# Dealing the taps of a depthwise convolution differently between a projection's products, with state stores issued later and filler products of other widths

## The chip, the cores and the metric

The kernel runs on one core of a Trainium2 chip. The metric is the device time of one execution in microseconds (us); lower is better. The kernel before takes 1147.51 us (median of 3 runs, 1146.17 to 1147.53).

## What is computed

One layer of a decoder trunk, for a prompt of 1024 tokens and 8 sample tokens, so N = 1032 columns of D = 1024 channels:

```
h = rmsnorm(x, norm1_g) * (1 + sc1) + sh1          # sc, sh, g come from silu(c) @ w_ada + b_ada
z = h @ w_in;  u, gb, gc, v, ga, gg = split(z)     # widths 256, 384, 384, 384, 384, 384
ya = pool_mix(u)                                   # causal means over 2, 4, 8, 16 rows, small product
yb = gb * causal_dwconv(gc * v, width 3)
yc = silu(layernorm(causal_dwconv(ga * sigmoid(gg), width 31) + conf_b))
x = x + g1 * (concat(ya, yb, yc) @ w_out)
h = rmsnorm(x, norm2_g) * (1 + sc2) + sh2
x = x + g2 * (square(relu(h @ w_ff1)) @ w_ff2)
y = rmsnorm(x, final_g)
```

The last rows of u, of gc * v and of ga * sigmoid(gg) are stored as new states.

## The kernel before, in words

Activations lie transposed in SBUF: channels on the 128 partitions, 1032 tokens on the free axis, in three column tiles of 344 (`TW`). A matrix product is made in float32r with both operands split in a high and a low part: for each block of 128 input channels three products (high by high, high by low, low by high), each over 3 tiles, so 9 matmuls of 128x344 per block. `product` (L1224 to L1235) does this; the two PSUM halves of `acc` (three banks each) take the chunks in turn, so a product may start when the chunk two before it was read.

`plan()` fixes the order of the units (one unit is one load of 128 weight columns). First gg and ga for c = 0, 1, 2; then u for c = 0, 1; then v, gc, gb for c = 0, 1, 2; then the output projection in two parts: `p1` (8 units of 5 blocks, over ya and yb) and `p2` (4 units of 3 blocks by two, over yc). Behind that come the second norm and the feed-forward part. The weights of a unit go from DMA to `wraw`, from there by ACT to `whi` (`high`, L531) and by POOL to `wlo` (`low`, L456): one ACT and one POOL instruction for each unit. ACT may do that for unit u + 2 when the product of unit u has ended.

Between the products of one round of ga there are also the products that make the modulation (`modulate`, L1367, from `ada` and `cT` into `modps`). DVE copies `modps` away (`mod_to_rows`, L791); the first `modulate` of the next round waits for that copy. PE then transposes it (L1377) and DVE adds the bias (`mod_finish`, L800).

What DVE does for each unit is written out by hand in the loop from L974 on:
- ga: glu = product times sigmoid (L981, L984), which also frees the chunk.
- u: `pooled` (L911 to L929), `ya_low` (L939).
- gc: product times v, and the convolution of width 3 (L1011 to L1022) into `wk[2]`.
- gb: yb = product times `wk[2]` (L1026). ACT rounds it to `yab_hi` (L633), DVE subtracts to get `yab_lo` (L1029).

The convolution of width 31 is the filling between these. It has 96 steps, in `steps`: for each of 3 channel blocks one start with bias (L886), 30 taps of one multiply-add over some 1000 columns (L892), and one addition for the samples (L896). `convolve(n)` does the next n steps, in order, from where it stands. Its calls give the dealing: 14, 14, 7 behind ga; 4, 4 behind u; 7 behind each v; 5 behind each gc; 6, 6 and all the rest behind gb. After the last, DVE adds the three blocks up (L1034, L1035) for the mean of the layernorm.

The first `p1` product reads the five blocks of ya and yb in order; its block 4 is yb of c = 2, and before it PE waits for the `yab_lo` of that block:

```
if kind == "p1":
    if c == 0:
        ready = lambda k: pe.wait_ge(ylo_ready, k + 1)
```

On ACT, in the turn of `p1` with c = 5, stand 16 DMAs that store the new states (L638 to L648), ahead of the three copies that make `yc_hi` (L653). DVE makes `yc_lo` from it (L1064), for `p2`.

At the second norm PE has little to do: it sums squares over the partitions with matmuls of one column (`token_sums`, L1265), spreads the reciprocal roots over the partitions (`spread`, L1294), and waits. Between these stand filler products whose result is never read (`keep_clock`, L1275): `WARM = (7, 12, 23)` of them, each 128x344, all into the bank `modps`, in the three places given by

```
norm_sums(3, WARM[0])
keep_clock(WARM[1])
spread(3, CHUNK_AT["norm2"])
keep_clock(WARM[2])
```

`WARM[0]` lies between the two halves of the token sums, `WARM[1]` ahead of the spread, `WARM[2]` behind it.

Of the kernel before, what the change touches and what calls it, by code (L numbers as in the profile page):

```python
# [8 lines left out]
ACT = mybir.ActivationFunctionType  # L9
AX_X = mybir.AxisListType.X  # L10

P = 128
# [5 lines left out]
TW = N // NT  # L18
# [3 lines left out]
POOL_C, CONV_C = 2, 3  # L22
# [79 lines left out]
COLS_AHEAD = 3  # L102


WARM = (7, 12, 23)
LAG = 2
SQ = {2: 0, 3: CONV_C, 4: CONV_C + KD}
ADDED = {2: 0, 3: 1, 4: KD - 1}
# [2 lines left out]
def decoder_trunk(nc, x_prompt, x_sample, c_prompt, c_sample, state_pool, state_sconv, state_conf,  # L111
# [11 lines left out]
    with ctx:  # L123
# [145 lines left out]
        def tiled(ap):  # L269
            return ap.rearrange("p (t w) -> p t w", t=NT)  # L270
# [231 lines left out]
        def _(act):  # L502
# [84 lines left out]
            for u in range(U_FF):  # L587
                (kind, c), n = UNITS[u]
                ps = flat(chunk_of(n))
                if kind == "p2":  # L590
                    squares(3, 2 * c, FREED_V[CHUNK_AT[("p2", 2 * c)]])
                if kind == "p1" and c == 2:
                    for j in range(CONV_C):
                        act.wait_ge(centred, j + 1)
                        nc.scalar.activation(wk[j][:], dc[:, j, :], ACT.Square).then_inc(sq_ready, 1)
                if kind == "p1" and c == LN_ROOT:
                    root(2)
                if kind == "p1" and c == 5:
                    for j in range(CONV_C):
                        act.wait_ge(ln_scaled, j + 1)  # L600
                        if j == 2:
                            act.wait_ge(silu_ready, 1)
                        nc.scalar.activation(wk[1 + j % 2][:], dc[:, j, :], ACT.Sigmoid,
                                             bias=lbT[:, j:j + 1]).then_inc(lsig_ready, 1)
                high_of(u + 2)
                if kind == "gg":
                    if c:
                        act.wait_ge(glu_ready, c)
                    nc.scalar.activation(tiled(wk[2]), ps, ACT.Sigmoid).then_inc(sig_ready, 1)
                if kind == "gg" and c == 2:  # L610

                    act.dma_start(ns_pool[0, :, 0:PBUF - 1, :], state_pool[0, :, 1:PBUF, :]).then_inc(old_stored, 16)
                    act.dma_start(ns_sconv[0, :, 0:SK - 2, :], state_sconv[0, :, 1:SK - 1, :]).then_inc(old_stored, 16)
                    act.dma_start(ns_conf[0, :, 0:CK - 2, :], state_conf[0, :, 1:CK - 1, :]).then_inc(old_stored, 16)
                if kind == "u":
                    nc.scalar.activation(last_cols[:, 0, 23 * c:23 * c + 23],
                                         chunk_of(n)[:, 2, TW - 23:TW], ACT.Copy).then_inc(last_u, 1)
                    if c == 1:
                        act.wait_ge(pool_ready, 1)
                    nc.scalar.activation(tiled(wk[c]), ps, ACT.Copy).then_inc(u_ready, 1)  # L620
                    if c == 1:
                        ya_high(0)
                if kind == "v":
                    if c == 0:
                        act.wait_ge(pool_ready, 2)
                    else:
                        act.wait_ge(ylo_ready, POOL_C + c)
                    nc.scalar.activation(tiled(wk[0]), ps, ACT.Copy).then_inc(v_ready, 1)
                    if c == 0:
                        ya_high(1)  # L630
                if kind == "gb":
                    act.wait_ge(yb_ready, c + 1)
                    nc.scalar.activation(yab_hi[:, POOL_C + c, :], wk[0][:], ACT.Copy).then_inc(yhi_ready, 1)  # L633
                if kind == "p1" and c == 5:
                    act.wait_ge(states_ready, 1)
                    for j in range(POOL_C):
                        r, cols = 23 * j, slice(j * P, (j + 1) * P)
                        act.dma_start(np_pool[0, 0, :, cols], states_out[r:r + PBUF, 0, :]).then_inc(new_stored, 16)  # L638
                        act.dma_start(ns_pool[0, :, PBUF - 1, cols], states_out[r + PBUF:r + 23, 0, :]
                                      ).then_inc(new_stored, 16)  # L640
                    for j in range(CONV_C):
                        r, cols = 46 + 10 * j, slice(j * P, (j + 1) * P)
                        act.dma_start(np_sconv[0, 0, :, cols], states_out[r:r + 2, 0, :]).then_inc(new_stored, 16)
                        act.dma_start(ns_sconv[0, :, SK - 2, cols], states_out[r + 2:r + 10, 0, :]
                                      ).then_inc(new_stored, 16)
                        r = LASTC * j
                        act.dma_start(np_conf[0, 0, :, cols], states_out[r:r + CK - 1, 1, :]).then_inc(new_stored, 16)
                        act.dma_start(ns_conf[0, :, CK - 2, cols], states_out[r + CK - 1:r + LASTC, 1, :]  # L648
                                      ).then_inc(new_stored, 16)
                if kind == "p1" and c == 5:  # L650
                    for j in range(CONV_C):
                        act.wait_ge(silu_ready, j + 1)
                        nc.scalar.activation(yc_hi[:, j, :], dc[:, j, :], ACT.Copy).then_inc(yhi_ready, 1)  # L653
                if kind == "p2":
                    squares(3, 2 * c + 1, FREED_V[CHUNK_AT[("p2", 2 * c + 1)]])

# [69 lines left out]
        def _(dve):  # L726
# [248 lines left out]
            for u in range(U_FF):  # L975
                (kind, c), n = UNITS[u]
                ps = flat(chunk_of(n))
                if kind == "ga":
# [5 lines left out]
                    nc.vector.tensor_tensor(tiled(glu[:, c, :]), ps, tiled(wk[2]), ALU.mult).then_inc(glu_ready, 1)  # L984
                    if c == 2:
                        mod_to_rows(2)
                    convolve(14 if c < 2 else 7)
                if kind == "gg" and c == 1:
                    mod_to_rows(1)
                if kind == "gg" and c == 2:  # L990
# [1 line left out]
                if kind == "u":  # L992
# [5 lines left out]
                    pooled(c)  # L998
                    if c == 1:
                        ya_low(0)  # L1000
                    convolve(4)
                if kind == "v":
                    if c == 0:
                        ya_low(1)
                    convolve(7)
                if kind == "gc":
                    dve.wait_ge(psum_full, n + 1)
                    dve.wait_ge(v_ready, c + 1)
# [11 lines left out]
                        link(nc.vector.scalar_tensor_tensor(out[:, s:T], cv[:, 0:T - s], tap[2 - s], out[:, s:T],  # L1020
                                                            ALU.mult, ALU.add))
                    link(nc.vector.tensor_tensor(out[:, T:N], out[:, T:N], past_sconv[:, c, :], ALU.add))  # L1022
                    convolve(5)
                if kind == "gb":
                    dve.wait_ge(psum_full, n + 1)
                    nc.vector.tensor_tensor(tiled(wk[0]), ps, tiled(wk[2]), ALU.mult).then_inc(yb_ready, 1)  # L1026
                    dve.wait_ge(yb_ready, c + 1)
                    dve.wait_ge(yhi_ready, POOL_C + c + 1)
                    nc.vector.tensor_tensor(yab_lo[:, POOL_C + c, :], wk[0][:], yab_hi[:, POOL_C + c, :].bitcast(F32),  # L1029
                                            ALU.subtract).then_inc(ylo_ready, 1)  # L1030
                    convolve(6 if c < 2 else 200)
                    if c == 2:
                        dve.wait_ge(conv_step, done)
                        link(nc.vector.tensor_tensor(wk[1][:], dc[:, 0, :], dc[:, 1, :], ALU.add))  # L1034
# [161 lines left out]
        def _(pe):  # L1196
# [73 lines left out]
                return nc.tensor.matmul(tps[0:S, KD:R], rows, ones[:, 0:1], start=False, stop=stop,  # L1270
                                        skip_group_check=True)

            def keep_clock(count):
                for _ in range(count):
                    nc.tensor.matmul(modps[:, 0:TW], yc_hi[:, 0, 0:P], yc_hi[:, 0, 0:TW], start=True, stop=True)  # L1275

            def norm_sums(n, warm):

# [326 lines left out]
```

## Time and profile before

| | us |
|---|---|
| median of 3 runs | 1147.51 |
| lowest and highest | 1146.17, 1147.53 |
| span of the profiled execution, first to last instruction | 1144.4 |
| median less that span | 3.1 |
| PE busy | 1105.7 (97%) |
| DVE busy | 531.5 (46%) |
| POOL busy | 255.7 (22%) |
| ACT busy | 244.6 (21%) |
| mean granted clock of TensorE | 0.983 |

The page gives for the profiled execution the span, and no device time of its own beside it; the time around the span is taken as the 3.1 us to the median. In all views times count from the start of the span. An engine's busy share is over the whole program; the stages differ. From 0 to about 70 us inputs and modulation arrive, from 70 to 264 us run the products of the input projection, from 264 to 375 us the output projection with the layernorm, from 375 to 393 us the second norm, and from 393 us to the end the feed-forward part and the output.

### The profile page before, as it was taken

What the parts mean: (1) busy time and instruction counts of PE and PEld (TensorE: products, weight loads), DVE (VectorE), ACT (ScalarE), POOL (GpSimd) and SP (SyncE); (2) the same over time, 40 slices, a digit from 0 to 9 for tenths busy, and PEclk for the clock granted to TensorE, in tenths of its full rate; (3) what the DMA queues carried; (4) which work ended last, traced back from release to release, by engine and by line L of the source; (5) the groups of instructions that cost most, each with busy time, mean ns of one, the idle gap of its engine ahead of it and who ended that gap; (6) DMA issues with size and microseconds to landing.
All of it is one profiled execution on the core that took longest, in us unless ns stands there. A gap on an engine that the chain in (4) does not pass through costs nothing.

```text
span 1144.4 us, 16468 instructions
## 1 busy us (share of the span) xinstructions
PE 1105.7 (97%) x7055; PEld 1075.7 (94%) x7055; DVE 531.5 (46%) x670; ACT 244.6 (21%) x269; POOL 255.7 (22%) x190
## 2 busy tenths in 40 slices
PE   6899999996999999999999999999999999999996
PEld 5688889996999899999999999999999999999996
DVE  5897699999566742132222133222222223222355
ACT  6321121110233432211210211220221120122111
POOL 2731122121122212222221222121212121212200
PEclk8899999998999899999999999999999999999999
DMA  9978211110111111111111111111111111111212
GB/s 282 321 287 313 54 38 40 53 35 13 47 46 54 35 38 56 38 56 37 56 38 57 38 56 37 56 37 57 38 56 38 56 38 56 38 56 38 74 50 99
DMA packets 97172, 83.15 MB, mean 73 GB/s; under 512 B 2663, under 2 KB 92718, under 8 KB 95039
## 3 DMA queue, kind: packets, MB, share of 16 engines
q1 hardware_dynamic: 96350, 80.87, 22.7%
q8 instruction: 59, 0.97, 0.3%
q10 hardware_dynamic: 417, 0.65, 0.2%
q0 software_dynamic: 336, 0.58, 0.2%
q14 instruction: 10, 0.08, 0.0%
HBM read 77.77 MB, written 4.81 MB: 72 GB/s over the span
## 4 chain that ended last, share of the span: by engine, by line
PE 83%; DVE 12%; issue 1%; DMA 1%; SPq 1%; ACT 1%; POOL 0%; DVEq 0%; POOLq 0%; ACTq 0%
PE acc L1233 70%; DVE dc L892 7%; PE acc L1254 4%; PE modps L1367 1%; DMA ada<-in_w_ada 1%; PE acc L1524 1%; PE acc L1522 1%; PE acc L1523 1%; PE modps L1345 1%; DVE work L1020 1%; DVE work L911 1%; PE tps L1265 1%; PE acc L1551 1%; DVE work L1174 1%; PE acc L1294 1%
## 5 line engine op out<-in xcount | busy, mean ns | idle before, releaser
L456 POOL TENSOR_TENSOR wlo<-wraw,whi 128x1024 fp32r<-128x1024 f32 (+2 forms) x89 | 210.3, 2363 | 794.8 <-ACT whi L531 794.8
L531 ACT ACTIVATE whi<-wraw 128x1024 fp32r<-128x1024 f32 (+2 forms) x89 | 90.9, 1021 | 673.7 <-PE acc L1233 635.6
L1233 PE MATMUL acc<-hhi,whi 128*128 128x344 f32 x1080 | 230.3, 322 | 2.4 <-issue 1.7
L1233 PE MATMUL acc<-hlo,whi 128*128 128x344 f32 x1080 | 228.9, 320 | 0.0
L1233 PE MATMUL acc<-hhi,wlo 128*128 128x344 f32 x1080 | 228.0, 319 | 0.0
L1233 PEld LDWEIGHTS acc<-hhi,whi 128*128 128x128 f32 x1080 | 181.2, 188 | 7.3 <-issue 7.1
L1233 PEld LDWEIGHTS acc<-hlo,whi 128*128 128x128 f32 x1080 | 182.6, 189 | 0.0
L1233 PEld LDWEIGHTS acc<-hhi,wlo 128*128 128x128 f32 x1080 | 180.1, 188 | 0.0
L948 DVE SCALAR_TENSOR_TENSOR xT<-acc,modT,xT 128x688 f32<-128x688 f32 x72 | 67.2, 933 | 226.7 <-PE acc L1233 226.0
L1106 DVE SCALAR_TENSOR_TENSOR work<-acc,work 128x1032 f32<-128x1032 f32 x32 | 39.4, 1232 | 249.8 <-ACT work L667 249.8
L1233 PE MATMUL acc<-hid_hi,whi 128*128 128x344 f32 x672 | 142.2, 320 | 0.0
L1233 PE MATMUL acc<-hid_lo,whi 128*128 128x344 f32 x672 | 142.0, 319 | 0.0
L1233 PE MATMUL acc<-hid_hi,wlo 128*128 128x344 f32 x672 | 141.9, 319 | 0.0
L892 DVE SCALAR_TENSOR_TENSOR dc<-glu,tapT,dc 128x1023 f32<-128x1023 f32 (+14 forms) x90 | 134.5, 1495 | 2.9
L1233 PEld LDWEIGHTS acc<-hid_lo,whi 128*128 128x128 f32 x672 | 113.0, 188 | 0.0
L1233 PEld LDWEIGHTS acc<-hid_hi,whi 128*128 128x128 f32 x672 | 112.5, 188 | 0.0
L1233 PEld LDWEIGHTS acc<-hid_hi,wlo 128*128 128x128 f32 x672 | 112.4, 188 | 0.0
L1110 DVE TENSOR_TENSOR hid_lo<-work,hid_hi 128x1032 fp32r<-128x1032 f32 x32 | 39.5, 1233 | 39.1 <-ACT hid_hi L670 39.1
L670 ACT ACTIVATE hid_hi<-work 128x1032 fp32r<-128x1032 f32 x32 | 34.1, 1067 | 42.1 <-DVE work L1106 42.1
L950 DVE SCALAR_TENSOR_TENSOR xT<-acc,modT,xT 128x336 f32<-128x336 f32 x72 | 40.2, 558 | 0.0
L1233 PE MATMUL acc<-yab_hi,whi 128*128 128x344 f32 x120 | 27.2, 337 | 9.5 <-DVE yab_lo L1029 8.9
L667 ACT ACTIVATE work<-acc 128x1032 f32<-128x1032 f32 x32 | 32.5, 1015 | 0.0
(181 smaller groups left out, 982.2 us busy)
## 6 DMA issues: line engine op xcount, KB each, us to landing
wraw<-in_w_ff SPq DMA_DIRECT2D x64, 512.0 KB, 3.9
ada<-in_w_ada SPq DMA_DIRECT2D x16, 1024.0 KB, 8.2
wraw<-in_w_in SPq DMA_DIRECT2D x17, 512.0 KB, 4.7
ada<-in_w_ada SPq DMA_DIRECT2D x16, 512.0 KB, 7.4
xrow<-in_x_prompt SPq DMA_DIRECT2D x8, 512.0 KB, 8.6
out<-work SPq DMA_DIRECT2D x6, 512.0 KB
wraw<-in_w_out SPq DMA_DIRECT2D x8, 320.0 KB, 3.2
wraw<-in_w_out SPq DMA_DIRECT2D x4, 384.0 KB, 3.2
```

What stands on the lines that cost most here:

```text
L456: nc.gpsimd.tensor_tensor(o, a, b, ALU.subtract).then_inc(wlo_ready, 1)
L531: nc.scalar.activation(whi[:, slot, 0:n, :].rearrange("p k n -> p (k n)"), wraw[:, slot, 0:n * P], ACT.Copy).then_inc(whi_ready, 1)
L667: nc.scalar.activation(tiled(wk[0]), flat(acc[:, (C_FF + j) % 2, :, :]), ACT.Relu).then_inc(relu_ready, 1)
L670: nc.scalar.activation(hid_hi[:, slot + j, :], wk[1 + j % 2][:], ACT.Copy).then_inc(hid_hi_ready, 1)
L892: ins = nc.vector.scalar_tensor_tensor(dc[:, c, s:T], glu[:, c, 0:T - s], tapT[:, tap:tap + 1], dc[:, c, s:T], ALU.mult, ALU.add)
L911: link(nc.vector.tensor_tensor(dst[lo:P, PAD:PAD + T], src[lo:P, PAD:PAD + T], src[lo:P, PAD - w:PAD - w + T], ALU.add))
L948: nc.vector.scalar_tensor_tensor(pair(xT[:, d, 0:2 * TW]), ps[:, 0:2, 0:TW], g1, pair(xT[:, d, 0:2 * TW]), ALU.mult, ALU.add)
L950: nc.vector.scalar_tensor_tensor(xT[:, d, 2 * TW:T], ps[:, 2, 0:w2], g1, xT[:, d, 2 * TW:T], ALU.mult, ALU.add)
L1106: nc.vector.scalar_tensor_tensor(tiled(q), flat(acc[:, (C_FF + j) % 2, :, :]), 0.0, tiled(wk[0]), ALU.max, ALU.mult).then_inc(freed_v, 1)
L1110: nc.vector.tensor_tensor(hid_lo[:, slot + j, :], q[:], hid_hi[:, slot + j, :].bitcast(F32), ALU.subtract).then_inc(hid_lo_ready, 1)
L1233: last = nc.tensor.matmul(out[:, t, 0:TW], w[:, slot, b, :], x[:, k, t * TW:(t + 1) * TW], start=(i == 0 and w is whi and x is hi), stop=( ...
L1254: last = nc.tensor.matmul(outs[j][:, t, 0:TW], w[:, (u0 + j) % 2, k, :], x[:, k, t * TW:(t + 1) * TW], start=(k == 0 and w is whi and x is ...
```

## The change

Three edits.

1. The dealing of the convolution steps stands in a table `TAPS`: 19, 18, 9 behind ga; 4, 4 behind u; 7, 7, 2 behind v; 5, 5, 2 behind gc; behind gb, one step between yb and `yab_lo`, and then 5, 5 and the rest. The 96 steps and their order stay.
2. On ACT the 16 stores of the states are issued in the turn of `p1` with c = 7 and no more with c = 5; the copies to `yc_hi` stand in their old place, now without the stores ahead of them.
3. `keep_clock` takes a list of widths: 5 of 512; then 2 of 512, 10 of 258, 2 of 512; then 4 of 512, 8 of 172, 8 of 128, 8 of 512.

```diff
-WARM = (7, 12, 23)
+TAPS = {"ga": (19, 18, 9), "u": (4, 4), "v": (7, 7, 2), "gc": (5, 5, 2), "gb": (5, 5, CK + 1)}
+
+
+WARM = ((512,) * 5, (512,) * 2 + (258,) * 10 + (512,) * 2, (512,) * 4 + (172,) * 8 + (128,) * 8 + (512,) * 8)
@@ ScalarE, loop over the units
                 if kind == "p1" and c == 5:
+                    for j in range(CONV_C):
+                        act.wait_ge(silu_ready, j + 1)
+                        nc.scalar.activation(yc_hi[:, j, :], dc[:, j, :], ACT.Copy).then_inc(yhi_ready, 1)
+                if kind == "p1" and c == 7:
                     act.wait_ge(states_ready, 1)
                     for j in range(POOL_C):
...
-                if kind == "p1" and c == 5:
-                    for j in range(CONV_C):
-                        act.wait_ge(silu_ready, j + 1)
-                        nc.scalar.activation(yc_hi[:, j, :], dc[:, j, :], ACT.Copy).then_inc(yhi_ready, 1)
@@ VectorE, loop over the units
-                    convolve(14 if c < 2 else 7)
+                    convolve(TAPS["ga"][c])
...
-                    convolve(4)
+                    convolve(TAPS["u"][c])
...
-                    convolve(7)
+                    convolve(TAPS["v"][c])
...
-                    convolve(5)
+                    convolve(TAPS["gc"][c])
                 if kind == "gb":
                     dve.wait_ge(psum_full, n + 1)
                     nc.vector.tensor_tensor(tiled(wk[0]), ps, tiled(wk[2]), ALU.mult).then_inc(yb_ready, 1)
+                    convolve(1)
                     dve.wait_ge(yb_ready, c + 1)
                     dve.wait_ge(yhi_ready, POOL_C + c + 1)
                     nc.vector.tensor_tensor(yab_lo[:, POOL_C + c, :], wk[0][:], yab_hi[:, POOL_C + c, :].bitcast(F32),
                                             ALU.subtract).then_inc(ylo_ready, 1)
-                    convolve(6 if c < 2 else 200)
+                    convolve(TAPS["gb"][c])
@@ TensorE
-            def keep_clock(count):
-                for _ in range(count):
-                    nc.tensor.matmul(modps[:, 0:TW], yc_hi[:, 0, 0:P], yc_hi[:, 0, 0:TW], start=True, stop=True)
+            def keep_clock(widths):
+                for w in widths:
+                    nc.tensor.matmul(modps[:, 0:w], yc_hi[:, 0, 0:P], yc_hi[:, 0, 0:w], start=True, stop=True)
```

How this moves instructions is shown at three places. The changed kernel's lines are 3 or 4 further down than those of the kernel before (a tap is L892 before and L895 now). The width in a tap's row tells which tap it is: 1023 is the first of a channel block, 994 the last.

DVE behind the first ga, up to the second ga. The copy is `mod_to_rows`, for which PE's next `modulate` waits; `last_cols` is the first instruction that needs the second ga product. Before:

```order
L892 SCALAR_TENSOR_TENSOR dc<-glu,tapT,dc 128x1012
L892 SCALAR_TENSOR_TENSOR dc<-glu,tapT,dc 128x1011
L791 COPY work<-modps 128x512
L981 TENSOR_TENSOR last_cols<-acc,work 128x38
L984 TENSOR_TENSOR glu<-acc,work 128x1032
L892 SCALAR_TENSOR_TENSOR dc<-glu,tapT,dc 128x1010
```

Now:

```order
L895 SCALAR_TENSOR_TENSOR dc<-glu,tapT,dc 128x1011
L895 SCALAR_TENSOR_TENSOR dc<-glu,tapT,dc 128x1010
L895 SCALAR_TENSOR_TENSOR dc<-glu,tapT,dc 128x1009
L895 SCALAR_TENSOR_TENSOR dc<-glu,tapT,dc 128x1008
L895 SCALAR_TENSOR_TENSOR dc<-glu,tapT,dc 128x1007
L895 SCALAR_TENSOR_TENSOR dc<-glu,tapT,dc 128x1006
L794 COPY work<-modps 128x512
L984 TENSOR_TENSOR last_cols<-acc,work 128x38
L987 TENSOR_TENSOR glu<-acc,work 128x1032
L895 SCALAR_TENSOR_TENSOR dc<-glu,tapT,dc 128x1005
```

Five taps (1010 to 1006) now stand ahead of the copy and of the second ga's work.

DVE at the last gc and gb, up to the sums for the layernorm. `yab_lo` at its end is what PE waits for in the first `p1` product. Before:

```order
L892 SCALAR_TENSOR_TENSOR dc<-glu,tapT,dc 128x1002
L892 SCALAR_TENSOR_TENSOR dc<-glu,tapT,dc 128x1001
L892 SCALAR_TENSOR_TENSOR dc<-glu,tapT,dc 128x1000
L892 SCALAR_TENSOR_TENSOR dc<-glu,tapT,dc 128x999
L892 SCALAR_TENSOR_TENSOR dc<-glu,tapT,dc 128x998
L1026 TENSOR_TENSOR work<-acc,work 128x1032
L1029 TENSOR_TENSOR yab_lo<-work,yab_hi 128x1032
L892 SCALAR_TENSOR_TENSOR dc<-glu,tapT,dc 128x997
L892 SCALAR_TENSOR_TENSOR dc<-glu,tapT,dc 128x996
L892 SCALAR_TENSOR_TENSOR dc<-glu,tapT,dc 128x995
L892 SCALAR_TENSOR_TENSOR dc<-glu,tapT,dc 128x994
L896 TENSOR_TENSOR dc<-dc,past_conf 128x8
```

Now:

```order
L895 SCALAR_TENSOR_TENSOR dc<-glu,tapT,dc 128x996
L895 SCALAR_TENSOR_TENSOR dc<-glu,tapT,dc 128x995
L1029 TENSOR_TENSOR work<-acc,work 128x1032
L895 SCALAR_TENSOR_TENSOR dc<-glu,tapT,dc 128x994
L1033 TENSOR_TENSOR yab_lo<-work,yab_hi 128x1032
L899 TENSOR_TENSOR dc<-dc,past_conf 128x8
```

Two taps stand between the last gc and gb where five stood, and the last tap has moved ahead of `yab_lo`, between it and the multiplication that it depends on.

ACT at the stores, their end before:

```order
L644 DMA out<-states_out 8x128
L647 DMA out<-states_out 30x128
L648 DMA out<-states_out 8x128
L653 ACTIVATE yc_hi<-dc 128x1032 x3
L531 ACTIVATE whi<-wraw 128x768 x2
L560 ACTIVATE work<-xT 128x1024
```

Their start now (`whi` are the weights of coming units, the `work` behind the stores is the first square for the second norm):

```order
L534 ACTIVATE whi<-wraw 128x640
L640 ACTIVATE yc_hi<-dc 128x1032 x3
L534 ACTIVATE whi<-wraw 128x768 x2
L645 DMA out<-states_out 15x128
L646 DMA out<-states_out 8x128
```

The copies and two weight roundings have moved ahead of the stores.

## Rows read from the trace of the kernel before

**Rows 1.** The profile's first part: busy time of the engines.

```profile
PE 1105.7 (97%) x7055; PEld 1075.7 (94%) x7055; DVE 531.5 (46%) x670; ACT 244.6 (21%) x269; POOL 255.7 (22%) x190
```

**Rows 2.** PE's waits of 0.2 us and more in the projections: total, times, longest.

```profile
PE acc L1233 <- DVE yab_lo L1029: 8.9, 1, 8.9
...
PE acc L1441 <- DVE yab_lo L939: 1.2, 1, 1.2
...
PE acc L1233 <- DVE work L1026: 0.2, 1, 0.2
```

**Rows 3.** Chain that ended last, in order of time: start, length, what.

```profile
170.66 3.29 DVE dc L892
173.98 1.29 DVE dc L892
...
278.48 10.58 PE acc L1233 x54
```

**Rows 4.** Timeline of DVE, ga products: start, length, what [idle before, releaser].

```profile
100.26 0.20 DVE L981 TENSOR_TENSOR last_cols<-acc,work 128x38 f32<-128x38 f32 x1 [6.44 <-PE acc L1233]
...
129.36 0.20 DVE L981 TENSOR_TENSOR last_cols<-acc,work 128x38 f32<-128x38 f32 x1 [5.27 <-PE acc L1233]
...
143.03 0.50 DVE L800 TENSOR_TENSOR modT<-tps,vecT 128x36 f32<-128x36 f32 x4 [3.06 <-PE tps L1377]
```

**Rows 5.** Timeline of DVE, last gb product.

```profile
274.76 1.23 DVE L1026 TENSOR_TENSOR work<-acc,work 128x1032 f32<-128x1032 f32 x1
277.19 1.23 DVE L1029 TENSOR_TENSOR yab_lo<-work,yab_hi 128x1032 fp32r<-128x1032 f32 x1 [1.20 <-ACT yab_hi L633]
```

**Rows 6.** Timeline of PE, end of the last gb product and first `p1` product.

```profile
262.69 0.38 PE L1449 MATMUL tps<-ident,last_cols 128*128 128x128 f32 x2
...
268.94 0.64 PE L1233 MATMUL acc<-yab_hi,wlo 128*128 128x344 f32 x3
```

**Rows 7.** Timeline of POOL, weight subtractions with a DVE tap beside them.

```profile
169.49 3.38 POOL L456 TENSOR_TENSOR wlo<-wraw,whi 128x1024 fp32r<-128x1024 f32 x1 [11.06 <-ACT whi L531]
...
263.76 2.00 POOL L456 TENSOR_TENSOR wlo<-wraw,whi 128x640 fp32r<-128x640 f32 x1 [9.00 <-ACT whi L531]
```

**Rows 8.** Stretches: length, busy (count) of PE, PEld, DVE, ACT, POOL; clock; DMA.

```profile
269.40:278.40 9.00, 0.17 (x2) 0.00 (x0) 7.66 (x8) 1.06 (x1) 0.00 (x0) 0.66 0.00 0
278.50:282.40 3.90, 3.90 (x14) 3.90 (x15) 3.79 (x4) 0.74 (x1) 0.06 (x1) 0.50 0.00 0
282.60:288.80 6.20, 6.20 (x41) 6.17 (x40) 6.10 (x8) 0.00 (x0) 2.29 (x1) 1.00 0.18 53
...
378.10:384.80 6.70, 6.70 (x31) 6.66 (x30) 3.53 (x11) 1.14 (x2) 0.61 (x1) 0.50 0.28 78
```

**Rows 9.** Timeline of ACT, stores to second norm (ACTq: its DMA issues).

```profile
326.88 0.37 ACTq L638 DMA_DIRECT2D out<-states_out  x1
...
332.32 2.98 ACT L653 ACTIVATE yc_hi<-dc 128x1032 fp32r<-128x1032 f32 x3 [4.73 <-issue]
...
341.07 0.85 ACT L531 ACTIVATE whi<-wraw 128x768 fp32r<-128x768 f32 x1 [5.03 <-PE acc L1233]
346.79 1.06 ACT L560 ACTIVATE work<-xT 128x1024 f32<-128x1024 f32 x1 [4.87 <-DVE gate_s L952]
349.60 0.85 ACT L531 ACTIVATE whi<-wraw 128x768 fp32r<-128x768 f32 x1 [1.75 <-PE acc L1233]
```

**Rows 10.** Chain that ended last, second norm.

```profile
381.71 3.55 PE modps L1275 x12
385.26 1.75 PE acc L1294 x6
...
393.10 2.00 PE acc L1254 x11
```

**Rows 11.** Timeline of PE, the filler products behind the spread.

```profile
386.58 4.04 PE L1275 MATMUL modps<-yc_hi 128*128 128x344 f32 x23
```

**Rows 12.** Timeline of DVE, the last work ahead of the spread.

```profile
382.90 1.36 DVE L767 TENSOR_TENSOR work<-ident,rstd 128x384 f32<-128x384 f32 x3
```

## The prediction

> **What bounds the kernel now.** I read the busy times first. PE is busy 97% of the span and every other engine under half of it [rows 1], so time can be won only where PE waits or runs at its lower clock. The list of PE's waits then gives the place: one wait of 8.9 us for DVE's `yab_lo`, as large as everything else that PE waits for in the projections together; beside it 1.2 us for `yab_lo` of ya and 0.2 us for a yb [rows 2]. The timeline of PE says where it is: PE ended the last gb product at 262.69, did four of the five blocks of the first `p1` product up to 269.58, and went on at 278.48 [rows 3, 6]. The table of stretches shows what the wait cost beside itself: the granted clock fell to 0.50 (1.2 GHz) in it, and 14 matmuls of 128x344 took the 3.90 us behind it, where 41 took 6.20 us at 1.00 (2.4 GHz) [rows 8].
>
> Why was DVE late? Going back on the chain of waits from 278.48, nearly every piece down to the ga products is DVE's, and most are taps of the wide convolution [rows 3]. Its timeline explains it: behind the three ga products DVE stood idle 6.44, 5.27 and 3.06 us, waiting for PE [rows 4], and from there to `yab_lo` of the last gb it was never free for more than the 1.20 us of ACT's rounding [rows 5]. So taps were done too late while room for them lay earlier.
>
> **The dealing.** A tap costs 1.29 us plus some 0.02 to the next, say 1.31; one that meets a POOL weight subtraction costs 3.29 [rows 3, 7]. A start and an addition for the samples together cost about 1.0 (an estimate; the start is one pass over the same columns).
>
> Steps done up to the work for u: 35 before, 46 now. Steps up to the last `yab_lo`: 91 before, 95 now. In between lie 56 steps before (54 taps, an addition, a start) and 49 now (47 taps, an addition, a start). So 7 taps fewer, 9.2 us. The single step put behind each of three yb fills the wait of 1.20 for ACT [rows 5]: 3.6 us more. By its own work DVE would end the last `yab_lo` 12.8 us earlier, at 278.42 less 12.8 = 265.6.
>
> It can't, since the gb product ends at 262.69 [rows 6]. From there: yb 1.23, a tap 1.31, `yab_lo` 1.23 [rows 5], and ACT's rounding fits beside the tap: 266.5. PE wants it at 269.58. The wait of 8.9 us goes whole, with 3 us to spare: **-8.9**. With it goes the low clock behind it: the stretch of 3.90 us at half clock holds 1.95 us of work at full clock, so **-2.0**. The bounds of this term are 0, if the clock dips there for another reason, and 2.0.
>
> What do the 11 taps cost in the ga stage?
> - First ga: five taps, 6.55 us, into an idle time of 6.44 that ended at 100.26 [rows 4]. DVE's copy of `modps` (0.7 us, ahead of that idle time before) now ends just behind 100.3, and PE's next `modulate` waits for it: **+0.2**, from 0.1 to 0.5.
> - Second ga: 18 steps, but with an addition and a start among them: two taps more, a start and an addition, 3.6 us into 5.27 [rows 4]: 0.
> - Third ga: 9 taps in place of 5, a start and an addition: 4.2 us into 3.06 [rows 4]. DVE comes to the bias addition 1.1 us late. What is late next is the pooling and `yab_lo` of ya, for which PE waited 1.2 us already [rows 2]. Bounds 0 and 1.1; I take **+0.4**, as the pooling has to wait for ACT's copy of u anyway and part of the delay is lost in that.
> - The wait of 0.2 for yb of the second gb [rows 2]: DVE is 1 to 2 us earlier there, **-0.2**.
>
> Is DVE still in time with these 0.6? PE moves by as much, so the 3 us stay. POOL's subtraction for the second `p1` unit ran from 263.76 to 265.76 [rows 7], right where the tap and `yab_lo` now stand, and can hold DVE by up to 2.0: the spare time shrinks to 1. A tap there has begun or waits a whole POOL instruction: the tap of 3.29 us at 170.66 began while POOL's 3.38 us instruction ran [rows 3, 7].
>
> The Trainium skill, "SBUF — State Buffer", section "Who interferes with whom", says that a VectorE instruction with two SBUF inputs contends with a GpSimd instruction that reads SBUF, and that the second to start blocks until the first ends. By that rule each POOL instruction holds up one tap at most, so extra taps in the ga stage stay at their bare price; the trace agrees (one tap of 3.29 among neighbours of 1.29), and the rule speaks against the last rival below.
>
> For the layernorm, the three channel blocks are summed when the last tap is done: before 4 taps behind `yab_lo`, now only the addition. PE comes to it earlier by 11 us, DVE by as much, and with 5 us fewer to do. Among the PE waits that count there is none in that part [rows 2], and none should come.
>
> **The stores.** The 16 issues took from 326.88 to 332.32 on ACT [rows 9]. They move behind the weight rounding at 341.07, whose end is 341.92; 5.4 us later is 347.3, where the first square began at 346.79. So that square is 0.5 us late, ends at 348.4, and the next rounding waits for PE until 349.60 anyway [rows 9]. `yc_hi` and `yc_lo` come 5 us earlier, but no wait of PE hangs on them. Net **0**; if something did hang on the late square, at most 0.5.
>
> **The fillers.** Second group: 14 products with 4628 columns in place of 12 with 4128. Before, they ran at clock 0.50 [rows 8] and took 3.55 us [rows 10], and the spread began the moment they ended, 1.0 us after DVE had its last piece ready (382.90 + 1.36 = 384.26) [rows 10, 12]. At that pace the new ones take 3.98: **+0.4**. First group: 2560 columns for 2408, under 0.1. Third group: 8544 columns for 7912. Before, 4.04 us [rows 11] in the 6.1 us from 387.01, where the spread ended, to 393.10, where POOL's sample columns let PE go on [rows 10]; by columns 4.4 now, hidden: **0**. If the narrow ones cost as much as one of 344, 28 products take 4.9 and the 512 ones some 1 more, still hidden.
>
> **Sum.** -8.9 - 2.0 + 0.2 + 0.4 - 0.2 + 0.4 = -10.1. The profiled span of 1144.4 becomes 1134.3; with the 3.1 us that lie between it and the median, 1147.5 becomes **1137.4**. Own range: 1135.4 to 1139.4.
>
> **Rivals.**
> - *The clock falls elsewhere at the second norm.* It was at 0.50 from 378.1 to 384.8 [rows 8], behind token sums of one column. All this now comes 10 us earlier and with denser fillers. If the clock holds, 6.7 us at half clock shrink by up to 3: 1134.4. Against it: the token sums are as they were, and they come before the drop.
> - *A part of the wait stays.* If POOL's instruction and the chain yb, ACT, tap, `yab_lo` add up worse than above, PE waits 1 to 3 us at block 4, and may lose up to 1 more by the clock: about 1141. For it: a spare of only 1 us with POOL between. Against: 3 without.
> - *Fillers in the way.* If the clock is still 0.50 in the third group, 8544 columns at the pace of the second (4128 in 3.55 us) take 7.3 against 6.1 of room, +1.2; with narrow ones as dear as wide ones, up to +4: 1139 to 1142.
> - *The change doesn't do what it says.* DVE was late, but once it is not, another wait takes the 10 us in the layernorm, as PE runs into the centring and squares of DVE and ACT: 1147. Against it: their order and distance to PE are unchanged, and DVE has less in between.
> - *Slower.* One mechanism, in the first ga: if the five added taps each paid what the tap beside POOL paid (3.29), they would take 16.5 us against 7.0 of room (copy included), and PE would wait some 9.5 us for the `modps` copy, with 2.0 for the clock as behind the wait at 269.58. With the 10.1 gained: 1148.9. It decides when the extra taps run 17 us together. Against it: POOL has one such instruction in a product.
>
> **How the numbers follow.** Forecast 0.68, kinder clock 0.10, part of the wait 0.10, fillers 0.05, given back 0.05, slower 0.02. The predicted time is the forecast's. Left out below 1134 is some 0.05, above 1141.2 about 0.12, so the range is 1134.0 to 1141.2. A measurement of this kernel can tell some 0.2%, 2.3 us, from no change. Forecast, kinder clock, fillers and a part of the wait are all faster by more than that: 0.93; "given back" is mostly within 0.2%: 0.04; slower 0.03.
>
> **What would show it.** Right: PE's wait for `yab_lo` of yb gone and PE at clock 1.00 through the first `p1` products; DVE's waits at `last_cols` down from 6.4 and 5.3 to about 0 and 1.7; a wait of DVE for the last gb product of about 1 us, new; no idle time of DVE ahead of the tap behind yb; ACT's 4.73 us ahead of `yc_hi` gone. Wrong: a PE wait at the first `modulate` behind the second ga of over 1 us; a remaining wait at block 4; a spread that begins later behind its token sums than 3.6 us; new waits of PE inside the layernorm.

## The result

| | us |
|---|---|
| the kernel before, median of 4 runs | 1147.52 (1146.17 to 1149.13) |
| the changed kernel, median of 4 runs | 1137.45 (1134.78 to 1138.90) |
| ratio, 95% interval | 0.9903 (0.9887 to 0.9919) |
| span of the profiled executions | 1144.4 before, 1136.8 after |

The change takes 10.1 us off, 0.97%. The profiled execution of the changed kernel is the slowest of its four (1138.90, so 2.1 us lie around its span); it shows 7.6 us of the 10.1. In every run of the record 1.8 to 2.2 us lie around the span. So the profiled execution before, with its span of 1144.4, was about 1.0 us faster than the median, and the one after 1.4 us slower than its own; together these are the gap of 2.5 us, and the text below shows where in the program it arose. Three of the 57 runs of the kernel before in the experiments (1210, 1803 and 2178 us) were executions in a slow state, and the ratios leave them out.

### The profile page after: what moved, and what is told of

Read it like the earlier page. It is cut to its first block, busy times and chain, and to the rows that moved or that the text cites. A ratio compares the mean times of both kernels' runs of the same rounds, so it can differ in the third digit from the quotient of the medians.

```text
span 1136.8 us, 16478 instructions
## 1 busy us (share of the span) xinstructions
PE 1108.3 (97%) x7060; PEld 1078.0 (95%) x7060; DVE 531.0 (47%) x670; ACT 244.6 (22%) x269; POOL 255.5 (22%) x190
## 4 chain that ended last, share of the span: by engine, by line
PE 88%; DVE 7%; SPq 2%; issue 1%; DMA 1%; POOL 0%; ACT 0%; DVEq 0%; POOLq 0%
PE acc L1237 76%; PE acc L1258 4%; DVE dc L895 4%; SPq L346 1%; PE acc L1528 1%; PE acc L1526 1%; PE acc L1527 1%; PE tps L1269 1%; DMA ada<-in_w_ada 1%; PE modps L1371 1%; DVE work L914 1%; PE acc L1555 1%; PE modps L1349 1%; DVE work L1178 1%; PE modps L1279 1%
## 5 line engine op out<-in xcount | busy, mean ns | idle before, releaser
L895 DVE SCALAR_TENSOR_TENSOR dc<-glu,tapT,dc 128x1023 f32<-128x1023 f32 (+14 forms) x90 | 136.3, 1515 | 2.9
L1526 PE MATMUL acc<-hid_hi,hhi 128*128 128x344 f32 x96 | 31.2, 325 | 0.0
```

The costliest lines, as they stand in the source:

```text
L895: ins = nc.vector.scalar_tensor_tensor(dc[:, c, s:T], glu[:, c, 0:T - s], tapT[:, tap:tap + 1], dc[:, c, s:T], ALU.mult, ALU.add)
L1526: nc.tensor.matmul(bank[:, 0:TW], w_hi, hi[:, k, cols], start=(b == 0), stop=False)
```

## The profile after

PE's waits in the projections and the second norm, in the list of waits of the changed kernel (what waits, for whom: total, times, longest):

```profile
PE acc L1445 <- DVE yab_lo L942: 1.7, 1, 1.7
...
PE acc L1258 <- POOL hlo L479: 1.5, 1, 1.5
...
PE acc L1237 <- ACT work L623: 0.6, 1, 0.6
PE modps L1371 <- DVE work L794: 0.3, 1, 0.3
```

The 8.9 us for `yab_lo` of yb [rows 2] are gone, and so are the 0.2 us for yb. The 1.2 us for `yab_lo` of ya have become 1.7, and 0.3 us for the copy of `modps` is new.

The timeline of DVE in the changed kernel, at the ga products and at the last gb product (start, length, what, idle before and releaser):

```profile
100.14 0.69 DVE L794 COPY work<-modps 128x512 f32<-128x512 f32 x1
100.75 0.20 DVE L984 TENSOR_TENSOR last_cols<-acc,work 128x38 f32<-128x38 f32 x1
...
130.15 0.20 DVE L984 TENSOR_TENSOR last_cols<-acc,work 128x38 f32<-128x38 f32 x1 [1.90 <-PE acc L1237]
...
145.05 0.49 DVE L803 TENSOR_TENSOR modT<-tps,vecT 128x36 f32<-128x36 f32 x4
145.66 1.83 DVE L998 SCALAR_TENSOR_TENSOR A<-modT,vecT 128x72 f32<-128x72 f32 x1
...
258.27 2.55 DVE L895 SCALAR_TENSOR_TENSOR dc<-glu,tapT,dc 128x996 f32<-128x996 f32 x2
263.77 1.23 DVE L1029 TENSOR_TENSOR work<-acc,work 128x1032 f32<-128x1032 f32 x1 [2.95 <-PE acc L1237]
264.92 2.36 DVE L895 SCALAR_TENSOR_TENSOR dc<-glu,tapT,dc 128x994 f32<-128x994 f32 x1
267.20 1.22 DVE L1033 TENSOR_TENSOR yab_lo<-work,yab_hi 128x1032 fp32r<-128x1032 f32 x1
```

Idle times of 6.44, 5.27 and 3.06 us [rows 4] have become 0, 1.90 and 0. At the end DVE now waits 2.95 us for PE's last gb product, the reverse of before. The tap behind yb took 2.36 us in place of 1.3, since POOL's subtraction ran from 264.65 for 1.57 us; still `yab_lo` ended at 268.42, and PE came to that block at 269.46.

What PE did from there on, in the chain that ended last, of the changed kernel (start, length, what):

```profile
263.95 14.20 PE acc L1237 x90
278.15 1.73 PE acc L1460 x6
...
299.35 9.05 PE acc L1237 x45
308.40 1.73 PE acc L1298 x6
310.13 55.60 PE acc L1237 x351
...
365.81 1.92 PE tps L1269 x16
367.73 1.95 PE modps L1279 x5
369.68 3.21 PE tps L1269 x16
...
373.01 4.16 PE modps L1279 x14
377.17 2.37 PE acc L1298 x6
```

The same chain of the kernel before, for the pieces that stand against these:

```profile
289.05 1.85 PE acc L1456 x6
...
317.77 1.74 PE acc L1294 x6
...
375.19 1.92 PE tps L1265 x16
```

The mean for the layernorm (L1456, now L1460) begins 10.9 us earlier. At its spread (L1294, now L1298) 9.4 are left, at the token sums of the second norm still 9.4, at the last spread 8.1 (377.17 against 385.26, [rows 10]), at the end 7.6. So the gain came at one place, about as large as forecast, and then a part was lost at two, the two norms. Both hold stretches of low clock. The table of stretches of the changed kernel (length, busy and count of PE, PEld, DVE, ACT, POOL, clock, DMA):

```profile
368.20:378.20 10.00, 10.00 (x39) 8.83 (x38) 4.06 (x11) 1.65 (x3) 1.14 (x1) 0.50 0.18 52
...
296.50:303.10 6.60, 6.60 (x28) 6.56 (x29) 2.12 (x7) 0.21 (x1) 0.19 (x1) 0.50 0.20 52
263.70:277.90 14.20, 14.20 (x93) 14.20 (x92) 9.01 (x10) 2.55 (x3) 3.15 (x2) 1.00 0.17 46
```

The low stretch at the layernorm in the same table of the kernel before:

```profile
309.90:313.20 3.30, 3.30 (x14) 3.30 (x13) 1.55 (x4) 0.00 (x0) 0.00 (x0) 0.50 0.08 23
```

The first two output products ran wholly at clock 1.00. But at the second norm the low stretch is 10.0 us long, where it was 6.7 [rows 8], and at the layernorm's token sums 6.6, where it was 3.3. In this one execution, that is.

The timeline of ACT shows the stores and the square behind them:

```profile
331.72 0.36 ACTq L645 DMA_DIRECT2D out<-states_out  x1
...
336.80 0.33 ACTq L655 DMA_DIRECT2D out<-states_out  x1
337.42 1.06 ACT L563 ACTIVATE work<-xT 128x1024 f32<-128x1024 f32 x1 [4.88 <-DVE gate_s L955]
340.23 0.85 ACT L534 ACTIVATE whi<-wraw 128x768 fp32r<-128x768 f32 x1 [1.75 <-PE acc L1237]
```

The first issue is at 331.72 us, while ACT's weight rounding (331.70, 0.85 us) still runs, and the square stands 9.4 us earlier than before (346.79, [rows 9]), as all work around it.

## The experiments

Theory A: the dealing of the taps removes one wait and the low clock behind it, and the other two edits do nothing. Theory B: much of what single runs show is the length of the low stretches at the norms. Theory C: the new fillers bring a part by holding the clock. Each kernel was run with the kernel before on the same chip, in three rounds on three chips: the first four rows, the next four, the last four. Between rows of different rounds the ratios are the safer comparison.

| run | median us (runs) | kernel before | ratio, 95% interval |
|---|---|---|---|
| whole change | 1137.16 (6) | 1147.86 | 0.9906 (0.9888 to 0.9924) |
| taps alone | 1138.18 (6) | 1147.86 | 0.9916 (0.9899 to 0.9932) |
| fillers alone | 1148.04 (12) | 1147.86 | 1.0000 (0.9988 to 1.0013) |
| stores alone | 1147.68 (12) | 1147.86 | 1.0000 (0.9988 to 1.0012) |
| step between alone | 1145.08 (12) | 1148.38 | 0.9971 (0.9955 to 0.9986) |
| dealing alone | 1137.66 (6) | 1148.38 | 0.9912 (0.9891 to 0.9933) |
| first ga 23 | 1147.65 (12) | 1148.38 | 0.9992 (0.9977 to 1.0006) |
| short second group | 1136.60 (6) | 1148.38 | 0.9903 (0.9885 to 0.9922) |
| whole change again | 1138.41 (6) | 1148.33 | 0.9909 (0.9894 to 0.9925) |
| no fillers | 1139.02 (6) | 1148.33 | 0.9919 (0.9904 to 0.9935) |
| tuned taps | 1136.98 (6) | 1148.33 | 0.9901 (0.9885 to 0.9918) |
| tuned taps, short group | 1136.27 (6) | 1148.33 | 0.9893 (0.9877 to 0.9909) |

### The parts one by one

The whole change: 

> The whole change once more, for its spread beside the kernel before. Theory A (the dealing of the taps does it: the one wait of 8.9 us goes with the low clock behind it): about 1137 us, 10 us below the kernel before. Theory B (a good part of the gain is a matter of how long TensorE's clock is low at the norms, which moves from run to run): single times spread over 3 to 4 us, and rise as the mean granted clock falls, by about 1 us for each 0.001.

Taps alone:

```diff
+TAPS = {"ga": (19, 18, 9), "u": (4, 4), "v": (7, 7, 2), "gc": (5, 5, 2), "gb": (5, 5, CK + 1)}
...
+                    convolve(1)
```

> The new dealing of the taps alone; stores and fillers as before. Theory A: the wait at the fifth block of the first output product is gone, total 10.1 to 10.5 us below the kernel before (1137.0 to 1137.4). Theory C (the new fillers bring a part by holding the clock): 2 us or more slower than the whole change.

Fillers alone:

```diff
-WARM = (7, 12, 23)
+WARM = ((512,) * 5, (512,) * 2 + (258,) * 10 + (512,) * 2, (512,) * 4 + (172,) * 8 + (128,) * 8 + (512,) * 8)
```

> The new filler widths alone; taps and stores as before. Theory A: the second group runs at the low clock and holds the spread up 0.4 us longer: 0 to 0.5 us slower than the kernel before, not to be told from none. Theory C (fillers hold the clock): 2 to 3 us faster, with a shorter stretch at clock 0.50 behind the token sums.

Stores alone:

```diff
-                if kind == "p1" and c == 5:
+                if kind == "p1" and c == 7:
                     act.wait_ge(states_ready, 1)
```

> The stores issued in the turn of p1 with c = 7 alone; taps and fillers as before. Theory A: no difference, within 0.5 us; ACT's 4.7 us ahead of yc_hi are gone and the first square of the second norm begins about 0.5 us later. Rival: the earlier yc_hi and yc_lo let PE begin the p2 products sooner, some us faster.

The whole change repeated the 10 us; its six runs spread over 7.3 us, where 3 to 4 were expected. The taps alone gave 9.7 us. Its 1138.18 is 0.8 us above the 1137.0 to 1137.4 expected, and the intervals of "taps alone" and "whole change" lie nearly on one another. The fillers alone came out 0.2 us slower and the stores alone 0.2 faster, neither told from none. Theory A holds in size; theory C falls, as no 2 to 3 us appeared. The chain of "fillers alone" shows the term that was worked out for the second group:

```profile
382.86 3.98 PE modps L1278 x14
386.84 1.75 PE acc L1297 x6
```

3.98 us, as forecast, against 3.55 [rows 10], and the spread begins as it ends. That 0.4 us is there in the trace and too small to be seen in medians. In the trace of "stores alone" ACT no longer waits ahead of `yc_hi`, but the first square is not the 0.5 us late that was expected: it begins 0.2 us behind the copy of `gate_s` that it needs (347.21 against 347.02), as in the kernel before (346.79 against 346.60). The earlier `yc_hi` brought nothing, so the rival written there falls.

### Which part of the new dealing

The step between yb and `yab_lo` alone, on the old dealing:

```diff
+                    convolve(1)
                     dve.wait_ge(yb_ready, c + 1)
...
-                    convolve(6 if c < 2 else 200)
+                    convolve(5 if c < 2 else 200)
```

> On the kernel before, only one step of the convolution put between yb and yab_lo of each gb (the dealing stays otherwise: 14, 14, 7; 7; 5; then 5, 5 and the rest behind yab_lo). Theory A: DVE saves three waits of 1.20 us for ACT but does one tap of 1.31 us more ahead of the last yab_lo: 2.3 us less wait of PE (6.6 in place of 8.9), the low clock behind it stays: 1145.2 us. If the wait were another engine's doing, no gain.

The dealing alone, without that step (6, 6 and the rest behind gb):

> The new dealing, but no step between yb and yab_lo (6, 6 and the rest behind gb, as before). Theory A: 8 taps fewer ahead of the last yab_lo save 10.5 us, DVE stands at 268.5 to 269.5 us with it where PE wants it at 269.6 + 0.9: the wait is all but gone, 0 to 1 us left; within 1 us of the new taps with the step between. So the step between is spare time and no gain once the taps are dealt. Rival: each wait of 1.20 us counts, 3 us slower than with it.

The step alone gave 3.3 us by the medians (interval 1.6 to 5.2), where 2.3 was expected. In its trace the end of the last `yab_lo` came 13.3 us behind the end of the last gb product (275.08 less 261.79), where it was 15.7 before (278.42 less 262.69): 2.4 us, close to the 2.3. The low clock stayed. The timeline of PE in that run:

```profile
261.92 0.72 PE L1237 MATMUL acc<-yab_hi,whi 128*128 128x344 f32 x3
...
275.14 1.23 PE L1237 MATMUL acc<-yab_hi,whi 128*128 128x344 f32 x3 [7.31 <-DVE yab_lo L1033]
276.17 1.06 PE L1237 MATMUL acc<-yab_lo,whi 128*128 128x344 f32 x3
```

PE's wait shrank to 7.31 us and not to the 6.6 expected, because PE also began this product 0.8 us sooner behind its transposes; the first point of the part on why the prediction was right tells the reason.

The dealing alone gave 10.7 us, as much as the whole. Its DVE timeline shows why the step adds nothing to it:

```profile
263.48 1.23 DVE L1029 TENSOR_TENSOR work<-acc,work 128x1032 f32<-128x1032 f32 x1
265.90 1.23 DVE L1032 TENSOR_TENSOR yab_lo<-work,yab_hi 128x1032 fp32r<-128x1032 f32 x1 [1.20 <-ACT yab_hi L636]
```

`yab_lo` ends at 267.13, 1.8 us ahead of PE, which came to that block at 268.93; 268.5 to 269.5, with up to 1 us of wait, had been expected. It is also 1.3 us before that of the whole change: 0.5 of this is PE, which ended the last gb product at 263.04 in place of 263.57, and the rest is that no tap is held up by POOL between. The step and the new dealing do not add: once the dealing has brought DVE ahead of PE, the step only makes spare time.

### How full the first idle time is

```diff
-TAPS = {"ga": (19, 18, 9), ...
+TAPS = {"ga": (23, 14, 9), ...
```

> The whole change with 23, 14, 9 taps behind ga in place of 19, 18, 9: four steps more ahead of the modps copy, four fewer behind the second ga. Theory A: PE waits 4 x 1.31 = 5.2 us more for the copy at about 101 us (0.3 before, so 5.5), and the time rises by 5.2 us, plus up to 1.5 us where the clock falls in that wait. Rival (the first product's idle time of DVE is not the limit): no more than 1 us.

It cost 10.5 us against the whole change of the round before (1147.65 against 1137.16), 9.9 by the ratios, far more than the 5.2 to 6.7 expected: the direction was right and the size not. PE's wait and what followed, in its timeline of PE and its table of stretches:

```profile
108.22 5.13 PE L1371 MATMUL modps<-ada,cT 128*32 128x512 f32 x24 [7.63 <-DVE work L794]
```

```profile
108.20:112.90 4.70, 4.68 (x24) 1.11 (x24) 4.63 (x4) 0.00 (x0) 0.00 (x0) 0.50 0.36 96
```

The wait grew from 0.3 to 7.6 us, not to 5.5. The timelines of DVE in the changed kernel and in this one show the missing 2: 18 taps took 25.58 us, 22 took 32.94, which is 7.36 for four.

```profile
74.64 25.58 DVE L895 SCALAR_TENSOR_TENSOR dc<-glu,tapT,dc 128x1023 f32<-128x1023 f32 x18
```

```profile
74.53 32.94 DVE L895 SCALAR_TENSOR_TENSOR dc<-glu,tapT,dc 128x1023 f32<-128x1023 f32 x22
```

Its timeline of POOL names what they met:

```profile
102.77 2.34 POOL L459 TENSOR_TENSOR wlo<-wraw,whi 128x1024 fp32r<-128x1024 f32 x1 [11.55 <-ACT whi L534]
```

The second ga product ended at 100.6 us, ACT rounded the next weights at 101.64, and POOL's subtraction followed at 102.77. The taps that now stand there, ahead of the copy, meet it. (In the changed kernel it came at 102.95, behind the copy.) And the 24 products behind the wait took 5.13 us at clock 0.50, where they took 2.78 (100.97 to 103.75) in the changed kernel: 2.4 more. 5.2 + 2.1 + 2.4 = 9.7, against 9.9 or 10.5 by the medians. So the place holds 19 steps with 0.3 us of wait: four more undo the whole change.

### The second norm and its clock

A short second group:

```diff
-WARM = ((512,) * 5, (512,) * 2 + (258,) * 10 + (512,) * 2, ...
+WARM = ((512,) * 5, (512,) * 4, ...
```

> The whole change with a second filler group of 4 x 512 (2048 columns in place of 4628). Theory A: the group ends at the low clock 2.2 us sooner than 4.16 us, and the spread begins as soon as DVE has its pieces ready, 1.5 to 2 us earlier: 1.5 to 2 us faster. Rival (the fillers are needed to bring the clock back): the clock stays at 0.50 one stretch longer, into the feed-forward products, and it is 0 to 2 us slower.

The whole change again, with no edit:

> The whole change again, as the yardstick for the other three kernels of this round: 1137 us, single times between 1132 and 1139 with the granted clock between 0.992 and 0.983.

No fillers:

```diff
-WARM = ((512,) * 5, (512,) * 2 + (258,) * 10 + (512,) * 2, ...
+WARM = ((), (), ())
```

> The whole change without any filler product. Theory A (fillers only pay where they bring the clock back for the feed-forward part): the spread begins 2 us sooner, but TensorE enters the feed-forward products at clock 0.50 and stays there for 3.4 to 6.8 us, which costs 1.7 to 3.4 us: 0 to 2 us slower than the whole change. Theory C (fillers hold the clock over the whole norm): 4 us or more slower. If fillers only stand in the way: 2 us faster.

The short second group came out 0.6 us below the whole change, which ran in another round (ratios 0.9903 and 0.9906): a gain is not shown. Its trace does show the mechanism (the group takes 2.0 us in place of 4.2, the spread follows at once, and the first feed-forward products ran at clock 1.00, so the rival falls), but the median does not carry 1.5 to 2 us.

The whole change again came out at 1138.41, 1.4 us above the 1137 expected, with single times up to 1139.72.

Without any filler it is 0.6 us above the whole change of the same round and 1.5 above the median of all 16 runs of the changed kernel (1137.51). The intervals overlap, so a gain from all 47 fillers together is not told from none; it may be 1 us or so, and not the 4 or more of theory C. The table of stretches of the run without them:

```profile
370.30:387.30 17.00, 9.02 (x29) 6.99 (x30) 11.56 (x17) 6.16 (x9) 5.17 (x5) 0.50 0.10 31
```

17 us at the low clock and not 10, but 8 of them idle: PE waits there for DVE and for POOL's sample columns (1.9 and 6.1 us), and where PE has nothing to do the low clock takes no time from it. It costs where it reaches past 384 us into the feed-forward products, 3.3 us of them at half clock; what the absent second group no longer holds up makes up for most of it.

Theory B is borne out by the single runs. The changed kernel's 16 runs lie between 1131.81 (mean granted clock 0.992) and 1139.72 us (0.985; the five longest 0.983 to 0.985), and a straight line through them gives 0.74 us for each 0.001 of clock, correlation -0.89; 54 runs of the kernel before in the same rounds give 0.84 and -0.86. About 1 us for each 0.001 was expected. The mean clock does not say where the clock was low, and it also counts the first 50 us; for that a pair of traces is needed. The fastest of the 16 was profiled; its table of stretches beside the two above:

```profile
293.00:303.00 10.00, 10.00 (x76) 9.91 (x75) 3.61 (x10) 2.23 (x3) 1.53 (x1) 1.00 0.13 34
...
366.90:370.20 3.30, 3.30 (x14) 3.02 (x14) 2.00 (x7) 0.21 (x1) 0.00 (x0) 0.50 0.49 142
```

The same program, at the same place: no low clock at the layernorm, and 3.3 us of it at the second norm where the other execution had 10.0. Its span is 1129.7 against 1136.8. Of these 7.1 us, 1.0 was there when the layernorm's mean began (277.14 against 278.15), from the stage of the inputs; when the feed-forward products began it was 7.2 (378.43 against 385.63). So some 6.2 us arose at and between the two norms.

### A version with the places filled better

```diff
-TAPS = {"ga": (19, 18, 9), "u": (4, 4), "v": (7, 7, 2), ...
+TAPS = {"ga": (18, 19, 8), "u": (4, 4), "v": (8, 7, 2), ...
```

> The whole change with 18, 19, 8 taps behind ga, 4, 4 behind u and 8, 7, 2 behind v: one tap less ahead of the modps copy and one less ahead of the pooling of u. Theory A: PE's wait of 0.3 us for the copy goes, and the wait of 1.7 us for yab_lo of ya shrinks to 0.3 to 0.9 us, with no new wait at the last yb: 1.1 to 1.6 us faster than the whole change, about 1135.8. Rival: DVE comes 1.3 us later to yb of the second gb, for which PE then waits, and nothing is won.

> The dealing of the run before together with a second filler group of 4 x 512. Theory A: another 0.5 to 1.5 us below it, as the spread begins about 2 us sooner where the clock is low there and 0.5 us sooner where it is high: about 1135. Rival: the clock comes back later and nothing is won.

The tuned taps were 1.4 us below the whole change of the round (1136.98 against 1138.41), the short group took off another 0.7, where 0.5 to 1.5 was expected; each is within its interval, and with both together, 2.1 us, the intervals still overlap. The trace of the tuned taps has no PE wait for the copy of `modps` any more, and this for ya, as before the change:

```profile
PE acc L1445 <- DVE yab_lo L942: 1.1, 1, 1.1
```

0.3 to 0.9 us had been expected for ya. In the traces PE needed 192.65 us from its first `modulate` beside the ga products (69.71) to the end of the last gb product (262.36) and 193.19 in the changed kernel, so these places explain 0.5 us of the 1.4; the rest is not explained by them. The version with the short group has the lowest median of all, 0.9893 of the kernel before; that it is faster than the whole change is not shown.

## Why the prediction was right, point by point

- **The wait of 8.9 us and the low clock behind it, -10.9.** Both went; the layernorm's mean began 10.9 us earlier, although PE came 0.9 later to the end of the last gb product (263.57 against 262.69). So the stretch itself saved 11.8: 8.9, about 2 for the clock, and 0.8 by which PE now starts the first output product sooner behind its transposes. The last was not in the sum. Before, PE started at 263.65, 0.58 us behind the transposes. This product is written to the PSUM half that the last gc product had filled, and the program lets it start when DVE has read that; DVE, late here too, was done at 263.54 (262.32 + 1.22). From the timelines of PE and DVE of the kernel before:

```profile
263.65 0.71 PE L1233 MATMUL acc<-yab_hi,whi 128*128 128x344 f32 x3 [0.58 <-issue]
```

```profile
262.32 1.22 DVE L1014 TENSOR_TENSOR work<-acc,work 128x1032 f32<-128x1032 f32 x1
```

  The view writes "issue", but in the run of the step alone DVE had read that half at 260.14 (258.92 + 1.22), ahead of the transposes, and PE began 0.13 us behind the start of its transposes (261.92 against 261.79), as in the changed kernel (263.70 against 263.57):

```profile
258.92 1.22 DVE L1017 TENSOR_TENSOR work<-acc,work 128x1032 f32<-128x1032 f32 x1
```

  So the late DVE made PE wait at two places, and the list of waits showed only the second.
- **The ga and gb stage, +0.2 + 0.4 - 0.2 = +0.4.** PE was 0.9 late at its end, but 0.5 of that was there before any instruction that the change moves, in the stage of the inputs: PE's first `modulate` beside the ga products began at 69.90 before and at 70.38 now. That start moves by itself; in two more profiled executions of the changed kernel it lay at 69.36 and at 70.66. From there to the end of the last gb product PE took 192.79 us before and 193.19 now: +0.4, as forecast. The next three points are its parts (by their waits 0.3 + 0.5 - 0.2 = 0.6; where the other 0.2 was made up is not looked into).
- **+0.2 at the first ga.** Measured 0.3, of PE's wait for the copy. The rival "slower" named this place: it is real (23 steps there undo everything), but one more tap met POOL and not each, and the low clock cost 2.4 us in place of 2.0.
- **+0.4 at the third ga.** Measured 0.5 (1.7 less 1.2). The working named only the taps; the trace adds that the multiplication that makes `A2` (L998, shown as `A`) now runs beside POOL's subtraction and takes 1.83 us. Part of the delay was lost in the wait for ACT, as said.
- **-0.2 at the second gb.** The wait is gone.
- **Spare time at the last gb.** 3 us, or 1 with POOL between: POOL did come between, and 1.0 was left (269.46 less 268.42). DVE's new wait for PE was put at 1 us and was 2.95; that guess stands in the list of signs and is not a term of the sum.
- **Stores, 0.** Alone 1147.68 against 1147.86. The working had the 16 issues begin behind the end of the weight rounding and the square 0.5 us late. In the trace they begin beside the rounding, and the square, at 337.42, was not late at all. The net of 0 holds.
- **Fillers, +0.4.** In the trace of fillers alone 3.98 us, as predicted; by the medians nothing. In the changed kernel the group took 4.16, so the spread began later behind its token sums than the 3.6 us which the prediction lists as a sign of being wrong. That sign was set wrongly: the prediction's own 3.98 would have set it off.
- **The 3.1 us around the span.** In every run 1.8 to 2.2 us lie there. The other 1.0 was that the profiled execution before was faster than its median. As the sum is a difference, the forecast of the median is not touched by it; for the profiled execution it means 1134.3 + 2.1 = 1136.4.
- **What the sum did not hold.** It was worked out on one execution. The span after is 1136.8 and not the 1134.3 worked out: 0.5 came from the stage of the inputs, the stretch at the output projection gave 0.9 more than its term, and 2.9 beside the 0.4 of the fillers were lost from the layernorm's mean to the end (10.9 less 7.6). There this execution had some 6.6 us more of low clock at the two norms. The rival "kinder clock" was written as another mechanism; it is the scatter of this kernel, in both directions. At the two norms together the clock was low for about 10 us in the profiled executions of the kernel before, of the fillers alone and of the stores alone, and for 3.4, 17 and 17 us in the three of the changed kernel.
- **Luck.** The mechanism and the place are shown. That the median agrees to 0.1 us is luck: the stretch at the output projection gave 0.9 us more than its term, the norms move single times by several us, and the measured ratio is known only to about 1.8 us either way.

## What to carry to other kernels

When filler work for one engine is dealt out by hand between the steps of another, list the idle time of the first engine behind each step and the first wait of the second: work belongs into the idle times ahead of the wait, and each place has a size (here 19 steps behind the first ga), past which the second engine waits. Two remedies for one wait need not add, as here; measure each alone. And where a clock may fall, compare medians of many runs, with the granted clock beside each, before a difference of less than 2 us is believed.

## What the runs showed that was not expected

- The same program ran between 1131.81 and 1139.72 us, and the granted clock orders the runs. Two executions differ by 3.3 against 10.0 us of low clock at one and the same place.
- Four taps too many cost some 10 us, twice their own time, as they brought one more meeting with POOL and a stretch at the low clock.
- Narrow products save little: the fillers of 172 and of 128 columns kept PE busy for 1.0 us for 8 each, and by their starts in the trace they follow one another every 0.11 us at clock 1.00, where those of 344 columns in the kernel before do so every 0.16. The groups of the changed kernel by form (count, busy us, mean ns):

```profile
L1279 PE MATMUL modps<-yc_hi 128*128 128x128 f32 x8 | 1.0, 273 | 0.0
L1279 PE MATMUL modps<-yc_hi 128*128 128x172 f32 x8 | 1.0, 271 | 0.0
```
